# Where the squares of a half-finished residual are summed: VectorE adds six of eight tiles, TensorE multiplies two by the constant matrix

## The reference, cut to what matters

```
x = x + 0.5 * ga1 * rms_norm_2(f, g_post_ff1)         # "post" norm, then the residual
h = modulate(rms_norm_2(x, g_pre_mix), sh2, sc2)      # "pre" norm of the next sub-block
rms_norm_2(x, g) = x * rsqrt(mean(x * x, axis=-1) + EPS) * g
```

## Time and profile before

| what | value |
|---|---|
| time, median of 3 runs | 2980.67 us (2975.33 to 2983.93) |
| the profiled execution's own time | 2980.5 us |
| its span | 2977.6 us |
| mean granted TensorE clock | 0.995 of full |
| TensorE busy | 2918.9 us, 98% of the span |
| VectorE busy | 1916.4 us, 64% |
| ScalarE busy | 1146.7 us, 39% |
| POOL busy | 377.2 us, 13% |

### The profile page before, as it was taken

One profiled execution on the slowest core, in us unless ns is written; L12 is line 12 of the kernel. 1 busy time (PEld: TensorE's weight loads), 2 busy tenths in 40 slices (PEclk: granted clock), 3 DMA queues, 4 the chain that ended last, 5 costly groups with the idle time before them and its releaser, 6 DMA issues.

```text
span 2977.6 us, 57380 instructions
## 1 busy us (share of the span) xinstructions
PE 2918.9 (98%) x23812; PEld 2628.4 (88%) x23812; DVE 1916.4 (64%) x3773; ACT 1146.7 (39%) x2043; POOL 377.2 (13%) x610
## 2 busy tenths in 40 slices
PE   9999999999999999999999999999999999999998
PEld 8877899999999998789999889887888896799997
DVE  5574576557777856647764767677636657685565
ACT  4655232232212235552323434344222233664353
POOL 0242433100000020324320000002100000000000
PEclk9999999999999999999999999999999999999999
DMA  6725766234555574247533444437723431134442
GB/s 207 213 52 141 181 148 169 72 143 156 187 198 174 191 212 135 62 132 191 142 121 110 160 142 160 146 137 202 191 89 135 149 121 51 58 116 158 145 173 90
DMA packets 119513, 428.69 MB, mean 144 GB/s; under 512 B 14248, under 2 KB 16680, under 8 KB 114264
## 3 DMA queue, kind: packets, MB, share of 16 engines
q1 hardware_dynamic: 67032, 261.52, 25.2%
q0 software_dynamic: 52224, 163.51, 20.7%
HBM read 414.35 MB, written 109.01 MB: 176 GB/s over the span
## 4 chain that ended last, share of the span: by engine, by line
PE 87%; DVE 5%; ACT 4%; issue 2%; POOL 1%; DMA 1%; SPq 0%; DVEq 0%; ACTq 0%; POOLq 0%
PE acc L1390 14%; PE acc L1391 13%; PE acc L1392 13%; PE acc L1852 5%; PE acc L1853 5%; PE acc L1854 5%; PE acc L2118 4%; PE acc L2119 4%; PE acc L2120 4%; ACT temps L2535 2%; PE acc L1720 2%; PE acc L1661 1%; PE acc L1425 1%; PE acc L1918 1%; PE acc L1897 1%
## 5 line engine op out<-in xcount | busy, mean ns | idle before, releaser
L2271 ACT ACTIVATE toep_r<-ring 128x1024 fp32r<-128x1024 f32 (+2 forms) x216 | 251.4, 1165 | 322.2 <-PE acc L1392 322.2
L1391 PE MATMUL acc<-normed_r,toep_r 128*128 128x264 f32 (+2 forms) x1120 | 356.9, 319 | 0.0
L2973 DVE TENSOR_TENSOR ring_r<-ring,toep_r 128x1024 fp32r<-128x1024 f32 (+2 forms) x212 | 287.7, 1358 | 95.9 <-ACT toep_r L2271 95.4
L1392 PE MATMUL acc<-work_r,ring_r 128*128 128x264 f32 (+2 forms) x984 | 323.7, 329 | 0.0
L1852 PE MATMUL acc<-residual_r,toep_r 128*128 128x264 f32 (+1 forms) x1024 | 300.2, 293 | 1.6 <-DVE mixed L3411 1.6
L1853 PE MATMUL acc<-normed_r,toep_r 128*128 128x264 f32 (+1 forms) x1024 | 291.5, 285 | 0.0
L1854 PE MATMUL acc<-residual_r,ring_r 128*128 128x264 f32 (+1 forms) x1024 | 290.3, 284 | 0.0
L1390 PE MATMUL acc<-work_r,toep_r 128*128 128x264 f32 (+2 forms) x828 | 268.6, 324 | 0.7 <-DVE ring_r L2983 0.6
L1391 PE MATMUL acc<-work_r,toep_r 128*128 128x264 f32 (+2 forms) x720 | 231.4, 321 | 0.0
L1391 PEld LDWEIGHTS acc<-normed_r,toep_r 128*128 128x128 f32 x1120 | 210.6, 188 | 14.5
L1390 PE MATMUL acc<-mixed_r,toep_r 128*128 128x264 f32 x704 | 202.8, 288 | 0.0
(11 more groups left out here) (638 smaller groups left out, 8138.9 us busy)
## 6 DMA issues: line engine op xcount, KB each, us to landing
ring<-in_w_pair SPq DMA_DIRECT2D x120, 512.0 KB, 3.4
sums_store<-in_w_pair POOLq DMA_DIRECT2D x80, 512.0 KB, 8.7
ring<-in_w_gb SPq DMA_DIRECT2D x64, 640.0 KB, 4.5
ring<-in_w_down SPq DMA_DIRECT2D x32, 704.0 KB, 4.0
lower_store<-in_w_pair POOLq DMA_DIRECT2D x20, 1024.0 KB, 9.9
sums_store<-sums_store POOLq DMA_DIRECT2D x40, 512.0 KB, 5.1
extra<-in_w_ada POOLq DMA_DIRECT2D x18, 1024.0 KB, 5.6
toep<-in_w_ada POOLq DMA_DIRECT2D x18, 1024.0 KB, 5.4
```

The source lines that it names most:

```text
L1391: mm(out, wh, xl[:, a:z], start=False, stop=False)
L1392: last = mm(out, wl, xh[:, a:z], start=False, stop=end)
L2271: A(high(ld), slot(ld), ACT.Copy).then_inc(S["w_high"], 1)
L2973: V.tensor_tensor(low(ld), slot(ld), high(ld), ALU.subtract).then_inc(S["w_low"], 1)
```

## The change

The "pre" norm of the first half (not of the second) gets a `total`, the tensor `upper`, which lies unused at both places. Four pairs of mean products become one, after job 10; VectorE gets six additions of 128x256 at each edge: those of tiles 1 and 2 after the residual of tiles 2 to 4, those of tiles 3 to 6 after the residual of tiles 5 to 7. ScalarE's squares stay in their order; the first goes to `upper`, and what they wait for changes.

```diff
-MEANS_IN, MEANS_AFTER = {KT + 1: (0, 1), KT + 2: (4, 5)}, {KT + 1: (2, 3), KT + 2: (6, 7)}
+SUMS_AT, MEANS_AFTER = {KT: (1, 2), KT + 1: (3, 4, 5, 6)}, {KT + 2: (0, KT - 1)}
...
                 if pre:
-                    e["pre"].append(norm(H, e["post"][-1]["done"], range(KT), [span], bank=7))
+                    e["pre"].append(norm(H, e["post"][-1]["done"], range(KT), [span], bank=7,
+                                         total=None if span is SPANS[1] else upper))
...
                 def inside(i):
                     if i == KT:
                         post_mean(e, 0)
-                    elif e["pre"]:
-                        pre_means(e["pre"][0], MEANS_IN.get(i, ()))
...
                     added(e["post"][0], g, TILES_AT.get(i, ()))
+                    if e["pre"]:
+                        for m in SUMS_AT.get(i, ()):
+                            summed(e["pre"][0], m)
```

## The result

| | before | changed |
|---|---|---|
| median | 2980.32 us (16 runs, 2972.48 to 2985.05) | 2984.57 us (16 runs, 2980.3 to 2987.8) |
| ratio | | 1.0016, 95% interval 1.001 to 1.0022 |
| span of the profiled execution | 2977.6 us | 2981.6 us |
| mean granted TensorE clock | 0.995 | 0.993 |

The loss is clear of noise, but under the 0.3% that the prediction took as the bound of "no change"; the time lies in the range (2976.5 to 2987.5) and 2.8 us above the forecast of 2981.8.

The account below looks back on a forecast made before the run. The prediction took TensorE to set the pace at the first edge and hardly at the second. First edge -0.7 us and second +1.8 us gave +1.1 us on 2980.67, so 2981.8 us, range 2976.5 to 2987.5.

Parts of the forecast that it names:

- The bound at each edge: TensorE sets the pace at the first edge, hardly at the second, where VectorE comes late.
- the 2.6 us of products: First edge: three of four pairs of mean products go from TensorE, at 0.86 us a pair.
- The new wait: TensorE's first mean product waits for VectorE's sixth addition, idling 1.85 us at the first edge, 4.7 at the second.
- the step from one addition to the next: On VectorE, each addition but the first waits for the one before: 0.42 + 0.04 = 0.46 us.
- What followed the second pair: Second edge: ScalarE's root comes 1.8 us late and the chain behind it all moves, +1.8 us.
- The clock: TensorE's clock stays at 1.00 in the 10 us behind each pair; forecast's chance 0.43.
- Rival 2: Clock falls in the new gap: 2984.5 us at the second edge alone, 2989.4 with both; chance 0.30.
- the term for the pair: Second edge, clock at half rate: the pair of mean products takes 0.9 us more, straight on the chain.
- Rival 1 (the additions fit): Additions and squares overlap so well that they cost nothing at either edge: -3.0 us, 2977.7 us; chance 0.17.
- Rival 3 (nothing comes through): Later waits take up the shift, or the two edges cancel: 2980.7 us; chance 0.10.

Follow-up runs that it names:

- e4: Changed kernel without VectorE's twelve additions, TensorE multiplying only tiles 0 and 7; distances between "post" means 17.22 and 18.65 us, ratio 0.9997 to the kernel before.
- e1: Changed kernel with unread idle products in TensorE's gaps, 4 at the first edge, 10 at the second; "post"-mean distances 19.57 and 21.20 us, ratio 1.0009 to before.
- e5: Changed kernel with VectorE's additions put between the residuals at both edges; distances between "post" means 18.85 and 21.55 us, ratio 1.0003 to the kernel before.
- e9: Kernel before, changed at the first edge only: VectorE adds tiles 1 to 4, TensorE multiplies the total and tiles 5 to 7; ratio 0.9992 to before.
- e2: Changed kernel with only the first edge changed, the second as before; distances between "post" means 21.10 and 19.12 us, ratio 1.0008 to the kernel before.
- e8: Kernel before with only the first edge changed, its additions put between the residuals; distances between "post" means 18.86 and 19.13 us, ratio 1.0007 to before.
- e7: Kernel before with only the second edge changed and ten idle products in its gap; "post"-mean distances 19.82 and 21.19 us, ratio 1.0003 to before.

## Why the prediction was right, and where it was off

**The bound at each edge: right.** TensorE was the bound at the first edge, since the 2.6 us of products that the prediction counted came out as 2.60 in e4. At the second edge the prediction said that taking products away would bring 0.4 us, and e4 has 0.46; that the two agree so closely is in part luck, since e4's figure has a fall of the clock in it.

**The new wait: right in kind, a little short in size.** Idle time of 1.85 and 4.7 us was forecast, counted from where the next product would have started, and 2.25 and 4.99 measured. The pair was to start 0.7 us earlier and 1.7 us later; it was 0.35 earlier and 2.01 later. The mis-sized term is the step from one addition to the next that waits for it: 0.46 us was taken, but two additions take 0.94, so the second starts 0.52 us behind the first, and the four took 2.01 us instead of 1.86. TensorE started 0.14 us behind the last addition instead of 0.08. And at the first edge the first two additions and the total behind them took 0.98 us where 0.80 was counted, so that job 9's result came out no earlier than before, and not 0.15 us earlier. Without the clock, the sum would have been -0.25 + 2.09 = +1.8 us (e1) where +1.1 was forecast. The rule of the Trainium skill weighed there ("VectorE: DVE Perf Modes", The DRAIN you can't avoid), that a semaphore after each operation costs nothing extra, does not hold in these rows: an addition that waits for the one before it starts after 0.52 us, and in e5 the next operation that need not wait starts 0.34 us behind an addition.

**What followed the second pair: right.** All of the pair's delay arrived at the second "post" mean (2.01 us and 2.09 in e1), as the chain of root, norm and tiles had no slack.

**The clock: the step that failed.** The forecast held it at 1.00 at both edges and gave its fall 0.30, "most of it at one edge". It fell at both, in the trace of every kernel that had these gaps. Of the 3.2 us between the forecast's +1.1 and the +4.3 of the distances, the clock is 2.5 and the later pairs are 0.7. Rival 2 was what happened, in the form that was left outside the range ("with both the kernel is at 2989.4"); that the time still came out inside is due to its price, which was too high at both: 4.9 us forecast and 1.52 measured at the first edge, 2.7 and 0.94 at the second. At the first edge two terms were too large: I let the pair and all 33 products of job 11 run slowly, while the pair ran mostly at the full rate and sixteen products at the half; and I took 0.24 us for a product at half rate, where the trace has 0.21. At the second edge the term for the pair was right and the rest was nothing. ScalarE's root, in the changed kernel and in e1:

```profile
2614.65 0.47 ACT L2238 ACTIVATE work<-acc,small 128x256 f32<-128x256 f32 x1 [1.05 <-PE acc L1471]
```

```profile
2606.03 0.47 ACT L2241 ACTIVATE work<-acc,small 128x256 f32<-128x256 f32 x1
```

It starts 2.08 us behind the pair's start (2612.57) with the clock down and 1.14 behind it (2604.89) with the clock up: 0.94 us, the 0.9 that rival 2 put on the pair and all that this edge lost by the clock. From the root to the second "post" mean it is 7.17 and 7.18 us, so the 1.8 us put on job 11 and the products behind it did not come. So the time's place inside the range is in part luck, as the fall at both edges had been left outside. It is luck, too, that rival 2's time for one edge, 2984.5, is the measured median: it has 2.7 us for one fall, where two falls cost 2.5. (The prediction's remark that this case alone reaches 8.9 us does not come out either: 2989.4 is 8.7 above 2980.67.)

The rule of the Trainium skill that stood beside that rival ("TensorE: Matmul & The Clock Gate", Why this matters for your kernels), that gaps between bursts of matmuls bring the clock down, holds here in kind: it fell behind or inside gaps of 2.00, 2.09, 4.19 and 4.83 us, and stayed up with 1.39 and 1.41 us. The gaps of 2.00 and 2.09 us are shorter than those that it warns of; here they were enough.

**Rival 1 (the additions fit)** fell at both edges: TensorE waited for VectorE at both. **Rival 3 (nothing comes through)** fell: +4.3 us in the edges, +4.0 in the span, +4.25 in the medians.

## What to carry to other kernels

When work is moved from the bounding engine to a helper, ask first when the bounding engine will come for the result, and only then whether the helper has idle time in total: here VectorE was idle for a third of the span and still late at both places. Cut the exchange where the last addition is done before the matmuls ask for it (e9: four tiles instead of six) and leave alone the place where the helper is already the bound. At the first edge a hole of some 2 us in a dense stream of matmuls cost 1.52 us in clock on top of 2.35 of waiting, so price the hole, and look at the granted clock behind it.

## What the runs showed of the hardware that was not expected

- A gap of 2.0 to 2.1 us in an otherwise dense stretch was enough for the clock to fall from 2.4 to 1.2 GHz in all three traces that had one of this size (changed kernel and e2 at the first edge, e4 at the second); 1.4 us was not, in two traces (e5, e8). These are single executions; that 1.4 us never brings it down is not shown. The fall cost 1.5 us behind the gap of 2.1 and 0.9 with the gap of 4.8, where it showed only in what the next engine waited for.
- The mean granted clock differs between executions of one and the same kernel, and the time with it: 2982.8 us on average at 0.993 and 2975.0 at 0.997, in 80 executions of the kernel before. Differences of a few us between single executions say little here.
- An addition of 128x256 that waits for the addition before it starts 0.52 us behind it; with an operation that need not wait for it behind it, an addition costs 0.34 us (e5).
- Idle products of 0.45 us each (20 records in 4.61 us) kept the clock up through a wait of 4.8 us (e1, e7), and were worth 2.5 us to the changed kernel in the distances.
